# A hybrid decoder block in fp32: the down projection by a seven-product scheme, with weight sums made earlier and kept in DRAM

## The reference

```python
hmix = rmsnorm(x, norm_mix_g)
proj = hmix @ w_in                                   # u_ssm, q, k, v, gate_a, gate_b
y_ssm = gelu(s5_scan(u_ssm, ...))                    # width 512
y_a = (y_ssm @ glu_w_val) * sigmoid(y_ssm @ glu_w_gate)
o_attn = three dilated window attentions, merged by softmax of their log sums
y_b = o_attn @ w_attn_up
mixed = (sigmoid(gate_a) * y_a + sigmoid(gate_b) * y_b) @ w_out
x = x + mixed
hf = rmsnorm(x, norm_ffn_g)
g_pre = causal_dwconv(hf @ ffn_w_gate, ffn_conv_w, ffn_conv_b)     # width 2816
ff = (gelu(g_pre) * (hf @ ffn_w_up)) @ ffn_w_down                  # (1024, 2816) @ (2816, 1024)
out = x + ff
```

## Time and profile before

| | |
|---|---|
| median of three runs | 1811.03 us |
| profiled execution | 1807.07 us, its span in the trace 1805.3 us |
| mean granted TensorE clock | 0.992 |
| busy: TensorE, weight load, VectorE, ACT, GpSimd | 1755.5, 1403.1, 983.3, 573.4, 810.6 us |
| matmuls | 8448 |

### The profile page before, as it was taken

How to read it: one execution, slowest core, us unless ns; L and a number is a source line. 1 busy time by engine, 2 the same in 40 slices (tenths; PEclk the granted TensorE clock), 3 DMA queues, 4 the chain that set the end, 5 groups by cost and what they waited for, 6 DMA issues and landing times.

```text
span 1805.3 us, 23423 instructions
## 1 busy us (share of the span) xinstructions
PE 1755.5 (97%) x8448; PEld 1403.1 (78%) x8448; DVE 983.3 (54%) x1482; ACT 573.4 (32%) x1105; POOL 810.6 (45%) x589
## 2 busy tenths in 40 slices
PE   8999999999999988999999999999999999999997
PEld 6777777777777766888888888788888888888786
DVE  6453544565364465443313324788878878534634
ACT  6653454455255521111412223533333333000000
POOL 7544454644444276661227633454554554222221
PEclk9999999999999989999999999999999999999999
DMA  4111311321231134445212344322322322445211
GB/s 176 36 42 43 106 55 42 107 60 42 79 82 48 37 106 130 112 119 164 88 47 94 105 144 171 114 97 70 98 76 70 102 73 93 162 141 186 88 52 47
DMA packets 70529, 167.01 MB, mean 93 GB/s; under 512 B 14432, under 2 KB 31968, under 8 KB 70448
## 3 DMA queue, kind: packets, MB, share of 16 engines
q1 hardware_dynamic: 58192, 154.27, 26.8%
q10 hardware_dynamic: 11792, 10.04, 2.0%
q0 software_dynamic: 464, 1.62, 0.2%
HBM read 132.13 MB, written 32.59 MB: 91 GB/s over the span
## 4 chain that ended last, share of the span: by engine, by line
PE 83%; DVE 6%; DMA 4%; POOL 2%; issue 2%; ACT 2%; SPq 0%; DVEq 0%; POOLq 0%; ACTq 0%
PE bank L964 13%; PE bank L966 13%; PE bank L965 13%; PE bank L1317 7%; PE bank L1319 7%; PE bank L1318 7%; PE bank L1375 4%; PE bank L1377 4%; PE bank L1376 4%; DMA ab<-wgt_scr 2%; PE bank L1099 2%; PE bank L1110 1%; DVE sp L1887 1%; PE bank L1083 1%; DMA raw<-in_wblocks 1%
## 5 line engine op out<-in xcount | busy, mean ns | idle before, releaser
L964 PE MATMUL bank<-hhi,whi 128*128 128x512 f32 x1024 | 420.2, 410 | 10.8 <-POOL wlo L687 3.7
L966 PE MATMUL bank<-hhi,wlo 128*128 128x512 f32 x1024 | 407.0, 398 | 0.0
L965 PE MATMUL bank<-hlo,whi 128*128 128x512 f32 x1024 | 406.6, 397 | 0.0
L687 POOL TENSOR_TENSOR wlo<-raw,whi 128x1024 fp32r<-128x1024 f32 (+1 forms) x84 | 197.1, 2346 | 410.4 <-DVE whi L1711 408.8
L964 PEld LDWEIGHTS bank<-hhi,whi 128*128 128x128 f32 x1024 | 194.7, 190 | 59.0 <-issue 7.1
L966 PEld LDWEIGHTS bank<-hhi,wlo 128*128 128x128 f32 x1024 | 194.5, 190 | 45.8
L965 PEld LDWEIGHTS bank<-hlo,whi 128*128 128x128 f32 x1024 | 195.1, 191 | 40.0 <-issue 0.2
L1496 ACT ACTIVATE sp<-sp,sd 128x128 f32<-128x128 f32 (+1 forms) x192 | 84.2, 440 | 115.9 <-DVE sd L1891 115.7
L937 POOL TENSOR_TENSOR plo<-st,phi 128x512 fp32r<-128x512 f32 x60 | 79.5, 1328 | 58.7 <-ACT phi L1623 57.5
L2167 DVE CAST fhi<-ff 128x1024 fp32r (+1 forms) x44 | 31.4, 715 | 125.5 <-PE bank L1377 125.5
L1711 DVE CAST whi<-raw 128x1024 fp32r<-128x1024 f32 (+1 forms) x84 | 67.5, 804 | 51.9 <-DMA raw<-in_wblocks 41.5
(11 more groups left out here) (300 smaller groups left out, 3796.0 us busy)
## 6 DMA issues: line engine op xcount, KB each, us to landing
raw<-in_wblocks SPq DMA_DIRECT2D x98, 512.0 KB, 3.7
pair<-in_wblocks SPq DMA_DIRECT2D x40, 512.0 KB, 4.8
ff_scr<-ffo SPq DMA_DIRECT2D x22, 512.0 KB, 5.9
ff<-ff_scr SPq DMA_DIRECT2D x22, 512.0 KB, 4.0
ab<-wgt_scr SPq DMA_DIRECT2D x16, 512.0 KB, 5.9
rt<-rt_scr SPq DMA_DIRECT2D x8, 516.0 KB, 6.7
x<-in_xT SPq DMA_DIRECT2D x8, 512.0 KB, 8.5
zb_scr<-zb SPq DMA_DIRECT2D x8, 512.0 KB, 3.5
```

The costliest lines, as they stand in the source:

```text
L687: pool.tensor_tensor(wlo[par][:, 0:cols], raw[par][:, 0:cols], whi[par][:, 0:cols].bitcast(F32), ALU.subtract).then_inc(lo_done, 1)
L964: nc.tensor.matmul(ps, a, x, start=start and k == k_list[0], stop=False)
L965: nc.tensor.matmul(ps, a, y, start=False, stop=False)
L966: last = nc.tensor.matmul(ps, b, x, start=False, stop=stop and k == k_list[-1])
```

## The change

The down projection's weights (2816 x 1024) are cut into quarters: inner rows into the lower and upper 11 blocks, output rows into halves of four tiles. The activations are cut into quarters: the same inner halves, and tokens into halves. Seven products `M_1` to `M_7` of quarters or of sums of quarters, each 11 steps long with 4 tiles of 3 matmuls per step, give the four quarters of the output by additions.

- The sums of weight quarters are made on GpSimd (`weight_sums`, four adds of 128 x 512 per inner block, 11 blocks). ACT's queue loads the two weight blocks (`load_rows`), and stores the two sums in `wsum_scr` (`store_sums`), with two buffers `ws`. The eight gate-A blocks carry sums 0 to 6, the first four GLU blocks 7 to 10.
- The down projection runs in 77 steps over rings of four buffers. Per step SP loads 256 KB of weights; ACT casts the activations and the weights; GpSimd makes the weights' remainder and VectorE that of the activations. VectorE makes sums of activation quarters in place, three steps ahead (`down_act_sum`), and the output's sums (`partial`, `finish_tile`, `last_base`, `last_tile`). Banks alternate between two sets of four. SP stores the output.
- The code is straight-line where it was a loop.

```diff
+NK = NF // 2
+STEPS = 7 * NK
+RING = 4
+D_AHEAD = 3
+M_1, M_2, M_6, M_7, M_5, M_4, M_3 = range(7)
...
+            dwhi = sb("dwhi", [P, RING, HT], F32R)
...
+        def dbank(q, m):
+            return bank[(3, 4, 5, 6) [m] if q % 2 == 0 else (7, 0, 1, 2)[m]][:]
+        def down_weight(t):
+            q, c = divmod(t, NK)
+            if q in (M_1, M_2, M_4):
+                rows = wblocks[116 + c + (NK if q != M_1 else 0)]
+            else:
+                rows = wsum_scr[0 if q in (M_6, M_7) else 1, c]
+            return half(rows, 1 if q in (M_4, M_7, M_5) else 0)
...
         @block.sync
+            def load_dw(t):
+                if t >= RING:
+                    sp_.wait_ge(dw_lo, t - RING + 1)
+                sp_.dma_start(dw_raw[:, t % RING, :], down_weight(t)).then_inc(dw_in[t % RING], 16)
...
+            for g, h, rows, t0 in ((4, 0, range(15, 22), 8), (5, 1, range(11, 15), 12),
+                                   (6, 1, (4, 15, 5, 16, 6, 17, 7, 18, 8, 19, 9, 20, 10, 21), 16)):
+                for i, f in enumerate(rows):
+                    extra.setdefault(t0 + (i // 2 if g == 4 else i), []).append((load_ff, g, [f], h))
+            for g, t0, step in ((0, 23, 3), (1, 46, 2), (2, 65, 2), (3, 60, 1)):
+                for m in range(4):
+                    extra.setdefault(t0 + step * m, []).append((load_x1r, g, m))
...
+            for t in range(RING + 3, STEPS):
+                load_dw(t)
+                for f, *args in extra.get(t, ()):
+                    f(*args)
...
         @block.gpsimd
+            def weight_sums(c):
+                pool.wait_ge(ws_in[c % 2], 32 * (c // 2 + 1))
+                a11, a21, a12, a22 = (half(ws[c % 2][:, k, :], d) for k in range(2) for d in range(2))
+                link(tt(a22, a21, a22, ALU.add))
+                link(tt(a21, a11, a21, ALU.subtract))
+                link(tt(a11, a22, a11, ALU.subtract))
+                tt(a12, a12, a11, ALU.subtract).then_inc(ws_done, 1)
             for m in range(KC):
                 lo(B_E2 + m + 1, (m + 1) % 2)
+                if m:
+                    weight_sums(m - 1)
             for m in range(KC):
                 lo(B_VG + m + 1, (m + 1) % 2)
+                if KC - 1 + m < NK:
+                    weight_sums(KC - 1 + m)
                 pool.wait_ge(zb_in, 16 * (m + 1))
...
         @block.tensor
+                nc.tensor.matmul(ps, a, x, start=c == 0, stop=False)
+                nc.tensor.matmul(ps, a, y, start=False, stop=False)
+                last = nc.tensor.matmul(ps, b, x, start=False, stop=c == NK - 1)
...
+            for t in range(STEPS - 2):
+                operands(t)
+                for m in range(4):
+                    last = down_tile_mm(t, m)
+                last.then_inc(down_used, 1)
...
         @block.scalar
+            def load_rows(c):
+                if c >= 2:
+                    act.wait_ge(ws_out[c % 2], 32 * (c // 2))
+                for k in range(2):
+                    act.dma_start(ws[c % 2][:, k, :], wblocks[116 + NK * k + c]).then_inc(ws_in[c % 2], 16)
+            def store_sums(c):
+                act.wait_ge(ws_done, c + 1)
+                for k in range(2):
+                    act.dma_start(wsum_scr[k, c], ws[c % 2][:, k, :]).then_inc(ws_out[c % 2], 16)
...
                     act.activation(half(zt[:, m, :], h), half(zt[:, m, :], h), ACT.Sigmoid).then_inc(sga_done, 1)
+                if m == 0:
+                    act.wait_ge(state_done, HP)
+                    act.wait_ge(m_in, 16 * CH * HP)
+                else:
+                    store_sums(m - 1)
+                load_rows(m)
...
+            def down_weight_hi(t):
+                act.wait_ge(dw_in[t % RING], 16 * (t // RING + 2))
+                if t >= RING:
+                    act.wait_ge(down_used, t - RING + 1)
+                act.activation(dwhi[:, t % RING, :], dw_raw[:, t % RING, :], ACT.Copy).then_inc(dw_hi, 1)
...
         @block.vector
+            def down_act_sum(t):
+                q, c = divmod(t, NK)
+                if q == M_6:
+                    if c in (0, 4):
+                        dve.wait_ge(ff_in[5 + c // 4], ff_in0[5 + c // 4] + 16 * (4, 14)[c // 4])
+                    link(TT(b12, b22, b12, ALU.subtract))
+                    TT(b11, b11, b12, ALU.add).then_inc(da_sum, 1)
...
+            def finish_tile(n):
+                q, m, h, x, tile = final_tile(n)
+                product_in(q, m)
+                if n % 4 == 0:
+                    dve.wait_ge(x1r_in[n // 4], 16 + 64)
...
+            for m in range(4):
+                at[26 + 3 * m] = finish_tile, m
+                at[37 + m] = partial, M_6, m
+                at[48 + m] = partial, M_7, m
+                at[58 + 2 * m] = finish_tile, 4 + m
+                at[65 + m] = last_base, m
+                at[70 + 2 * m] = finish_tile, 8 + m
+            for t in range(RING, STEPS):
+                if t + D_AHEAD < STEPS:
+                    down_act_sum(t + D_AHEAD)
+                down_act_lo(t)
+                if t in at:
+                    f, *args = at[t]
+                    f(*args)
```

More of the change, by code:

```diff
@@ new lines, in _ @@
+            sp_.wait_ge(lo_p, SLOTS * NU)
+            for t in range(RING):
+                load_dw(t)
+            unit(NU // 2 - 1, 1, last=True)
+            for p in range(2):
+                sp_.wait_ge(ff_out[p], 16 * 9)
+            sp_.wait_ge(prod, last_unit + I_A12)
+            load_ff(1, range(4, 8), 0)
+            sp_.wait_ge(prod, last_unit + I_S4)
+            load_ff(2, range(8, 11), 0)
+            load_ff(3, range(11, 15), 0)
+            for t in range(RING, RING + 3):
+                load_dw(t)
@@ L946, in _ @@
                         rest(i, 2 * i2 + p, p)
-            def lo_down(n, par):
-                pool.wait_ge(hi_done, n + 1)
-                pool.tensor_tensor(dlo[par][:], raw[par][:], dhi[par][:].bitcast(F32), ALU.subtract).then_inc(lo_done, 1)
-            with pool.Fori(0, 11) as j:
-                lo_down(B_D + 2 * j, 0)
-                lo_down(B_D + 2 * j + 1, 1)
+            for t in range(STEPS):
+                pool.wait_ge(dw_hi, t + 1)
+                pool.tensor_tensor(dwlo[:, t % RING, :], dw_raw[:, t % RING, :], dwhi[:, t % RING, :].bitcast(F32),
+                                   ALU.subtract).then_inc(dw_lo, 1)
         @block.tensor
@@ L1382, in _, with down_free @@
-            for mh in range(2):
-                i0 = 11 * mh
-                down(i0, mh, start=True, free=mh)
-                with pe.Fori(0, 4) as j:
-                    for q in range(2):
-                        down(i0 + 1 + 2 * j + q, (mh + 1 + q) % 2)
-                down(i0 + 9, (mh + 1) % 2)
-                down(i0 + 10, mh, stop=True)
+            def down_free(q, m):
+                if q == M_1 and m == 1:
+                    pe.wait_ge(copied, NU)
+                elif q == M_1 and m == 2:
+                    pe.wait_ge(cdone, SUMS * (NU - 1) + N_G0)
+                elif q == M_1 and m == 3:
+                    pe.wait_ge(cdone, SUMS * (NU - 1) + N_U2)
+                elif q == M_2 and m == 0:
+                    pe.wait_ge(ff_done, 2 * NF + 4)
+                elif q == M_6:
+                    pe.wait_ge(down_snap, m + 1)
+                elif q > M_6:
+                    pe.wait_ge(down_read, 4 * (q - M_7) + m + 1)
@@ new lines, in operands @@
+            def operands(t):
+                pe.wait_ge(dw_lo, t + 1)
+                pe.wait_ge(da_lo, t + 1)
+            for t in range(STEPS - 2):
[3 more added lines that the diff above has]
+                last.then_inc(down_used, 1)
+            for t in (STEPS - 2, STEPS - 1):
+                operands(t)
+            for m in range(4):
+                for t in (STEPS - 2, STEPS - 1):
+                    last = down_tile_mm(t, m)
@@ L1643, in unit @@
                 copy(s1_t[:], I_A11)
+                if last:
+                    for t in range(RING):
+                        down_act_hi(t)
+                    act.wait_ge(prod, SLOTS * u + I_S2)
+                    for t in range(RING):
+                        down_weight_hi(t)
                 next_cast(I_A11)
```

251 lines of the change are left out of this document (136 added, 115 removed).

## The result

| | before | after |
|---|---|---|
| median on the same chip | 1808.11 us (1804.33 to 1813.93) | 1829.2 us (1828.78 to 1829.77) |
| ratio, 95% interval | | 1.0114 [1.0082, 1.0146] |
| profiled execution, span | 1807.07, 1805.3 us | 1828.78, 1827.0 us |
| matmuls, mean granted clock | 8448, 0.992 | 8316, 0.979 |

A forecast was written before the change was run, and what follows sets the result against it. The prediction took TensorE to bound the gate stages, any wait there being lost time one for one. Gate stages +42 and down projection -26 give +16 us on the 1811 us median: 1827 us, range 1805 to 1842.

The forecast's parts named there:

- The down projection, -26 predicted: Down projection: matmuls 211, stalls and contention 14, end 4.9, sum 230 against 256.1 us now; 26 us less (21 to 30).
- (a): Down projection, step 23: TensorE waits because VectorE's M6 sums wait for the half rows of group 6; a stall of 5 us.
- (b): Down projection: VectorE's first finishing tile waits for four x1 half rows, issued late; a stall of 4 to 5 us.
- (c): Down projection, around the stalls and the M4 sums: VectorE's adds wait out GpSimd instructions; another 5 us.
- rival 3: Gate stages and down projection: the clock drops after stalls, five times 1.7 to 3.4 us, 8 to 17; 1840 us, chance 0.11.
- The first stall: Gate A, block 3: wlo stands behind four adds waiting for loads issued after ACT's sigmoids; TensorE waits 12.5 us.
- The rounds: Gate A after the first wait: stores, loads and adds take 13.6 us against 11.15; 25 us late by its end.
- the load round: Gate A: two stores and then two loads on ACT's queue before the next sums, taken as 8.0 us (7 to 8.8).
- GLU added 21.1 instead of 17: GLU blocks: GpSimd also mixes gates, needing 13.5 us per block for three more blocks; 42 us late at the stage's end.
- Rival 1: Gate stages: loads do not queue behind stores, landing in 4.8 to 5 us; +20 - 26 = -6, 1805 us, chance 0.18.
- Rival 2: Gate stages: the sums are hidden and the stages keep their length, only the down projection counts; 1785 us, chance 0.07.
- Rival 4: Down projection: VectorE and GpSimd block each other throughout, 3.4 instead of 2.75 us per step with sums; 1842 us, chance 0.06.

The follow-up runs named there:

- experiment 5: The kernel before with the weight sums made in the gate blocks but not stored, down projection as before: 1831.52 us, ratio 1.0133.
- experiment 8: The change rescheduled, all its work kept: sums behind a wlo needed sooner, rows loaded a round or more ahead, down projection loads earlier: 1771.55 us, ratio 0.9807.
- experiment 4: The changed kernel with the down projection's activation half rows and first x1 rows loaded earlier: 1816.12 us, 13.1 less than after.
- 9: The kernel of experiment 8 with two SBUF regions exchanged (hhi/hlo and raw/whi/wlo), order untouched: 1765.64 us, ratio 0.9767.

## Why the prediction came out right, point by point

- **The down projection, -26 predicted, -25.9 measured.** The mechanism was right, the agreement to 0.1 us is luck. The matmuls were put at 211 and are 924 x 0.2267 = 209.5. The stalls (a) and (b) stand at steps 23 and 27 and are 5.8 and 5.5 us where 5 and 4 to 5 were predicted; a third of 0.9 was not predicted. From the last matmul's start to the end it is 4.3 us (4.9). Term (c), 5 us of VectorE and GpSimd in each other's way, did not come: between the stalls steps run at 12 x 0.2267, and VectorE's operations of 1.77 us (the row at 1666.26) fall into slack that was there. In its place the lower clock behind the two stalls took 4.4 us, which the forecast had left to rival 3. Two errors of 5 us cancelled.
- **The first stall, 12.5 predicted, 10.7 measured, and 1.7 behind it in slow matmuls.** The place and the releaser were right, one reason wrong: the loads were not held by the sigmoids but issued at 874.79, 5.4 us sooner than I had them. So wlo was there at 888.9, 4 us sooner than predicted; the other 1.3 went to the adds, which took 6.8 us where 5.45 were predicted, the longest 2.12. TensorE was itself there 2.2 us sooner (878.2 instead of 880.4): 12.5 - 3.9 + 2.2 = 10.8.
- **The rounds, 13.6 predicted, 14.7 measured** (first adds at 896.11 and 954.79, four rounds apart). The adds were right (5.4). The term that was mis-sized is the load round: 9.3 on average in place of 8.0, since two stores ahead cost 4.5 (experiment 5), not 2.5 to 3.2. Gate A became 28.6 us longer instead of 25.
- **GLU added 21.1 instead of 17.** Here a second term was too small: from 992.56 on, with three blocks to go, GpSimd takes 14.2 us a block (`wlo` at 992.56, 1006.69, 1020.95, 1035.14) and not 13.5, because the first add of a sum takes 1.8 to 2.3 us and the third 1.6 instead of 1.29. Both stages: +49.7 against +42, inside the bound of 50 that a load round of 8.8 gave.
- **Sum.** +16 predicted, +21.7 measured between the spans, +21.1 between the medians of one chip. The median of before on this chip was 1808.1 instead of 1811.03, which hides half of the difference in the predicted 1827.
- **Rival 1** (the loads land 4.8 to 5 us after the sums, stores or not, 1805) is refuted by experiment 5: with the stores the landings are 4.5 us later. In the Trainium skill, page DMA: Bandwidth & Descriptors, section Queues, rings and completion order, every DMA engine takes the descriptors of one queue in ring order. By that rule, the traces of the change and of experiment 5 agree. Part of the 4.5 us can as well come from sharing with the stores, as SP's slower loads suggest; the place in the queue and the sharing weren't separated.
- **Rival 2** (sums hidden, 1785) fell in the change as written, at the place that it named, wlo of block 3: it came at 888.9 and TensorE was there at 878.2. With the sums behind that wlo (experiment 8) gate A hides them.
- **Rival 3** (clock): the sign that the prediction named for it came, a granted clock of 0.93 and 0.91 in the gate stages, but the cost there did not. Of the 13.6 us in slow matmuls all but 0.1 stand between two waits for GpSimd or for what hangs on it (the last such wait ends at 1039.38), and GpSimd itself waited only for DMAs from 879.78 to 1037.5; so a faster TensorE would only have waited longer. In the down projection, where no such wait follows, the 4.4 us are net: experiment 4 took away 9.6 us of waits and 3.9 of slow matmuls and gave 13.5.
- **Rival 4** is refuted by the unbroken 0.2267 us.

## What to carry to other kernels

Where an engine takes its instructions in order, added work is priced by what it waits for and by what stands behind it, not by its length: the same adds and transfers cost 50 us ahead of the urgent `wlo` and behind late loads, and 3 us with the loads early and the sums behind `wlo`. In a chain of store, load and compute, put the load a round ahead before anything else; here that alone took back 30 of the 50. A low granted clock cost something here only where no wait for another engine followed. And compare the distance of matmul starts between operand pairs in a trace; two levels of it are worth a look at the addresses.

## What the runs showed of the hardware that was not expected

- The distance between two 128x512 fp32r matmuls is 0.2267 us where the addresses of weights and activations in SBUF agree by 256 bytes, and 0.232 to 0.234 where they differ by 128 (the exception is thi with phi in 9). Shifting one boundary by 128 bytes took 21.5 us off the kernel before (1805.7 to 1784.2), and 19.3 off the rescheduled one (1771.6 to 1752.3).
- DMAs that stand in ACT's program behind two sigmoids and a table load were issued at 874.79, before the table load at 875.80; their position in the code did not hold them. The sigmoids' inputs had been ready since 857.
- Two 512 KB stores ahead of two 512 KB loads on one queue delay the loads by 4.5 us (9.5 against 5.0 from the end of the adds); in the same stretches a 512 KB load on another queue took 5.5 us instead of 3.7.
- After a wait of 10.7 us eight matmuls of TensorE are at the lower clock level (0.43 us apart), and cost 1.7 us. In the down projection 13 are, after 5.8 us of waiting, and cost 2.7; after 5.5 us of waiting it is 8, and 1.7.
